# All sixteen shift and scale sums of the first modulation on VectorE, low-part products one group later, and the third chunk's low weights on VectorE

## The chip, the cores and the metric

The kernel runs on one core of one Trainium2 chip. The metric is the device time of one execution in microseconds (us); lower is better. TensorE is PE in the profile, VectorE DVE, ScalarE ACT, GpSimd POOL, and SyncE (SP) issues the loads.

## The reference

One layer of a streaming encoder over 1024 tokens of width 1024, all in f32. What matters here is its beginning:

```
mod = silu(c) @ w_ada + b_ada            # six vectors of 1024: sh1, sc1, gt1, sh2, sc2, gt2
h   = rms_norm(x, g_pre_mix) * (1 + sc1) + sh1
zin = h @ w_in                           # 1024 x 3072, the combined input projection
```

After it come a gated depthwise convolution over 31 taps, a chunkwise gated recurrence of four heads, the output projection, and a SwiGLU feed-forward part with its own modulation. The change touches only what is quoted.

## The kernel before

**The start stage.** `x` lies as eight tiles of 128 tokens. For each block `kt` of 128 channels (eight of them) the kernel needs one column of scale and one of shift: the dot product of `silu(c)` with a tile of `w_ada` of 128 channels by 1024. A tile of scale is multiplied and summed by VectorE (`scale(kt)`, one instruction that also accumulates). A tile of shift is treated likewise by `shift(kt)` for kt 0, 4, 5, 6 and 7. For kt 1, 2 and 3 (`TURNED_SHIFTS`) the tile is stored the other way round in HBM, and TensorE makes the column with eight matmuls of one column each (`shift_by_columns`), into a PSUM bank. `scale_shift(kt)` then makes the gain `gs` and the bias `mod` of the block (both of one column).

**Groups.** The normalised x is turned by TensorE in sixteen groups (`turn_x(g)`, four transposes of 128x128 each), a group being one block of channels by half of the tokens. `GROUPS` orders them: g 0 to 2 are kt 0 to 2 for the first half of the tokens, g 3 to 5 the same for the second half, and from g 6 on both halves of kt 3, of kt 4, and so on. For each group ScalarE applies gain and bias from PSUM and then rounds to the high part (`full_and_high(g)`, which signals `hi_ready`), VectorE subtracts to get the low part (`low_half(g)`, which signals `h_ready`), and TensorE adds the group's products for the first two chunks of `w_in` into `pair[0]` and `pair[1]` (`project_group(g)`). A product of two f32 numbers is made of three matmuls of 512 columns: high by high, high weight by low x, low weight by high x; with two chunks that is six matmuls a group, all after `h_ready`.

**Order on each engine** is the order of the program. ScalarE makes the squares and root mean squares of the x tiles (`squares`), tiles 0 to 3 ahead of group 0, tile 4 behind group 1, tiles 5 to 7 behind group 2. VectorE scales each x tile by them (`normalise_x`). `other_vectors()` on VectorE copies the turned small vectors out of `bank(3)`, which is the half of `pair[1]` that the second half of the tokens uses; it brings `vec_ready` to 2. TensorE waits for `vec_ready` 2 ahead of group 3. GpSimd splits the first two chunks' weights and, behind them, the third's (`split_first`).

**After the start stage** TensorE goes straight on: `project_first()` is the third chunk of `w_in` (48 matmuls, into `pair[3]`), and then chunk by chunk the rest of the kernel.

Of the kernel before, what the change touches and what calls it, by code (L numbers as in the profile page):

```python
# [26 lines left out]
P = 128  # L27
# [54 lines left out]
TURNED_SHIFTS = (1, 2, 3)  # L82
# [111 lines left out]
def build(nc, t_in, out):  # L194
# [11 lines left out]
    with ctx:  # L206
# [26 lines left out]
        cond_col = keep("cond_col", [P, KT])  # L233
# [68 lines left out]
        shift_column = sem("shift_column")  # L302
# [100 lines left out]

        def column_bank(kt):

            return bank(1 if kt == TURNED_SHIFTS[0] else 7)

# [356 lines left out]
        def _(pool):  # L764
# [91 lines left out]
            for q in range(2):  # L856
                split_first(2, q)
# [169 lines left out]
        def _(act):  # L1027
# [20 lines left out]
            act.wait_ge(vec_ready, 1)  # L1048
            act.activation(cond_col[:, :], vec[:, ROW_C:ROW_C + KT], ACT.Silu).then_inc(cond_ready, 1)
# [35 lines left out]
            squares(range(4, 5))  # L1085
            full_and_high(2)
            squares(range(5, TT))
            for g in range(EARLY, 16):
                full_and_high(g)
# [353 lines left out]
        def _(dve):  # L1443
# [16 lines left out]
            def lower_bounds():  # L1460

                dve.wait_ge(cond_ready, 3)
# [28 lines left out]
            def scale_shift(kt):  # L1491
# [5 lines left out]
                turned_here = sum(n <= kt for n in TURNED_SHIFTS)  # L1497
                if kt in TURNED_SHIFTS:
                    dve.wait_ge(shift_column, turned_here)
                    src = column_bank(kt)[:, kt:kt + 1]  # L1500
                else:
                    dve.wait_ge(shift_summed, kt + 1 - turned_here)
                    src = sums0[:, 1, kt:kt + 1]
                dve.tensor_tensor(mod[:, kt:kt + 1], src, vec[:, ROW_BADA + kt:ROW_BADA + kt + 1], ALU.add
# [17 lines left out]

            def normalise_x(i):

                dve.wait_ge(ss_ready, i + 1)
                normalise(x0[:, i, :], x0[:, i, :], i, 0).then_inc(xs_ready, 1)
# [9 lines left out]
            low_half(0)  # L1536
            scale_shift(1)
            scale(2)
            low_half(1)
            scale_shift(2)  # L1540
            other_vectors()
            low_half(2)
            for i in range(4, TT):
                normalise_x(i)
            scale(3)
            low_half(3)
            scale_shift(3)
# [4 lines left out]
            scale_shift(4)  # L1552
            for kt in range(3, KT):
# [4 lines left out]
                if kt + 2 < KT:  # L1558
                    shift(kt + 2)
                    scale_shift(kt + 2)  # L1560
            dve.memset(u[:, 0:TAPS - 1], 0.0)
# [484 lines left out]
        def _(pe):  # L2046
# [29 lines left out]
            def project_group(g):  # L2076
# [4 lines left out]
                hi, lo = (ha_hi, ha_lo) if kt < 4 else (hb_hi, hb_lo)  # L2081
                pe.wait_ge(h_ready, g + 1)
# [366 lines left out]
```

## Time and profile before

| | |
|---|---|
| median of 3 runs | 1116.43 us (1115.89 to 1846.04) |
| the profiled execution, its time | 1116.59 us |
| its span | 1114.8 us |
| TensorE busy | 1086.9 us, 97% of the span |
| VectorE, ScalarE, GpSimd busy | 828.2, 491.6, 746.2 us |
| chain of waits, share of TensorE | 94% |
| data moved | 108.02 MB, mean 97 GB/s |

The span is the part of the time between the first and the last instruction of the trace. The busy times of the engines overlap.

### The profile page before, as it was taken

The page shows a single profiled execution, that of the slowest core. Times are in us where ns is not written, and L with a number is a line of the kernel's source. Part 1 is how long each engine was busy: PE and PEld are TensorE (multiplying, and loading weights), DVE is VectorE, ACT ScalarE, POOL GpSimd, SP SyncE. Part 2 cuts the span into 40 slices and gives each one's busy share as a digit, 9 for nine tenths or more (in the row PEclk, how much of TensorE's full clock was granted, in tenths as well). Part 3 has the DMA queues.
Part 4 walks back from the last instruction along what each step waited for, and adds up shares of the span by engine and source line. Part 5 has one row for each costly group of instructions (what it writes and reads, how often), then busy time and mean ns, then how long its engine had stood idle before and what let it go on. Part 6 is the DMA issues. An engine that isn't in the chain of part 4 may idle for free.

```text
span 1114.8 us, 14441 instructions
## 1 busy us (share of the span) xinstructions
PE 1086.9 (97%) x5091; PEld 903.9 (81%) x5091; DVE 828.2 (74%) x1173; ACT 491.6 (44%) x833; POOL 746.2 (67%) x643
## 2 busy tenths in 40 slices
PE   4999999999999999999999999999999999999996
PEld 4788888888878888888888888888888888888885
DVE  4977997979997885689675757575766666666658
ACT  4765474564743734345333333332333333332324
POOL 5559648566572820438977777777786868696966
PEclk9999999999999999999999999999999999999999
DMA  9633313331211481303222222222221212222227
GB/s 350 221 103 124 96 57 95 95 96 56 61 55 39 170 320 57 114 25 98 66 76 67 76 66 72 61 69 65 76 67 61 73 60 74 65 66 69 65 53 297
DMA packets 98794, 108.02 MB, mean 97 GB/s; under 512 B 6590, under 2 KB 76451, under 8 KB 98723
## 3 DMA queue, kind: packets, MB, share of 16 engines
q1 hardware_dynamic: 97264, 102.79, 28.6%
q10 hardware_dynamic: 1458, 4.31, 1.0%
q8 instruction: 41, 0.67, 0.3%
q14 instruction: 31, 0.25, 0.1%
HBM read 98.68 MB, written 8.40 MB: 96 GB/s over the span
## 4 chain that ended last, share of the span: by engine, by line
PE 94%; DVE 3%; DMA 1%; issue 1%; ACT 1%; SPq 0%; DVEq 0%; ACTq 0%
PE pair L2335 34%; PE pair L2132 23%; PE pair L2355 17%; PE pair L2244 8%; PE pair L2174 2%; PE pair L2298 2%; PE pair L2378 2%; PE pair L2089 1%; DMA x<-in_x 1%; PE pair L2169 1%; PE pair L2188 1%; PE pair L2061 1%; PE pair L2100 1%; PE pair L2190 1%; PE pair L2183 1%
## 5 line engine op out<-in xcount | busy, mean ns | idle before, releaser
L1931 DVE TENSOR_TENSOR yt<-yt,pair 128x512 f32<-128x512 f32 x264 | 176.0, 683 | 34.7 <-PE pair L2355 34.7
L1607 DVE SCALAR_TENSOR_TENSOR pair<-u,conv_w_col,pair 128x512 f32<-128x512 f32 x208 | 139.5, 746 | 2.1 <-ACT pair L1203 1.6
L922 POOL TENSOR_TENSOR raw_r<-raw,w_hi 128x512 fp32r<-128x512 f32 x68 | 96.2, 1415 | 65.2 <-ACT w_hi L1341 65.2
L822 POOL TENSOR_TENSOR ada<-ada,cond 128x256 f32<-128x256 f32 x96 | 78.5, 852 | 70.4 <-DMA ada<-in_w_ada 70.3
L2355 PE MATMUL pair<-w_hi,op_hi 128*128 128x512 f32 x280 | 109.0, 389 | 0.0
L2355 PE MATMUL pair<-w_lo,op_hi 128*128 128x512 f32 x280 | 109.0, 389 | 0.0
L2355 PE MATMUL pair<-w_hi,op_lo 128*128 128x512 f32 x280 | 108.9, 389 | 0.0
L931 POOL TENSOR_TENSOR w_lo<-w_lo_f,w_hi 128x512 fp32r<-128x512 f32 x70 | 95.1, 1359 | 0.0
L2335 PE MATMUL pair<-t_lo,w_hi 128*128 128x512 f32 x240 | 93.7, 390 | 0.0
L2335 PE MATMUL pair<-t_hi,w_hi 128*128 128x512 f32 x240 | 93.4, 389 | 0.0
L812 POOL TENSOR_TENSOR w_lo<-raw,w_hi 128x256 fp32r<-128x256 f32 x84 | 66.8, 826 | 27.6 <-ACT w_hi L1098 27.5
L1341 ACT ACTIVATE w_hi<-raw 128x512 fp32r<-128x512 f32 x68 | 42.5, 626 | 73.0 <-PE pair L2335 71.7
L2335 PE MATMUL pair<-hb_lo,w_hi 128*128 128x512 f32 x160 | 63.1, 394 | 0.0
L2335 PE MATMUL pair<-hb_hi,w_hi 128*128 128x512 f32 x160 | 62.6, 391 | 0.0
L2132 PE MATMUL pair<-ha_hi,w_hi 128*128 128x512 f32 x192 | 62.4, 406 | 0.0
L2335 PE MATMUL pair<-ha_lo,w_hi 128*128 128x512 f32 x160 | 62.3, 390 | 0.0
L2335 PE MATMUL pair<-ha_hi,w_hi 128*128 128x512 f32 x160 | 62.3, 389 | 0.0
L2132 PE MATMUL pair<-hb_hi,w_hi 128*128 128x512 f32 x192 | 62.0, 404 | 0.0
L2355 PEld LDWEIGHTS pair<-w_hi,op_hi 128*128 128x128 f32 x280 | 52.6, 188 | 11.4
L2355 PEld LDWEIGHTS pair<-w_lo,op_hi 128*128 128x128 f32 x280 | 52.6, 188 | 11.0
L2355 PEld LDWEIGHTS pair<-w_hi,op_lo 128*128 128x128 f32 x280 | 52.6, 188 | 11.0
L2132 PE MATMUL pair<-ha_lo,w_hi 128*128 128x512 f32 x192 | 59.5, 391 | 0.0
(338 smaller groups left out, 2955.2 us busy)
## 6 DMA issues: line engine op xcount, KB each, us to landing
ada<-in_w_ada SPq DMA_DIRECT2D x40, 512.0 KB, 4.8
raw<-in_w_ffn_in SPq DMA_DIRECT2D x56, 256.0 KB, 2.9
raw<-in_w_in SPq DMA_DIRECT2D x21, 512.0 KB, 4.8
w_lo_f<-in_w_ffn_out SPq DMA_DIRECT2D x40, 256.0 KB, 3.1
w_hi_f<-in_w_ffn_out SPq DMA_DIRECT2D x30, 256.0 KB, 3.1
x<-in_x SPq DMA_DIRECT2D x8, 512.0 KB, 10.2
raw<-in_w_out SPq DMA_DIRECT2D x8, 512.0 KB, 3.4
ada_late<-in_w_ada SPq DMA_DIRECT2D x8, 512.0 KB, 6.9
```

The lines of the kernel that those rows point to most:

```text
L812: i_ = pool.tensor_tensor(w_lo[:, g % WS, cols], raw[:, g % RAW, cols], w_hi[:, g % WS, cols], ALU.subtract)
L822: i_ = pool.tensor_tensor(ada[:, n % ADA_RING, cols], ada[:, n % ADA_RING, cols], cond[:, cols], ALU.mult)
L922: pool.tensor_tensor(place_part(at), place_full(at), place_part(GU_HIGH[m % 3]), ALU.subtract).then_inc(gu_low, 1)
L931: pool.tensor_tensor(place_part(at), place_full(at), place_part(DOWN_HIGH[d % 2]), ALU.subtract).then_inc(down_low, 1)
L1341: act.activation(place_part(GU_HIGH[m % 3]), place_full(WEIGHT_PLACES[e][k]), ACT.Copy).then_inc(gu_high, 1)
L1607: i_ = dve.scalar_tensor_tensor(out=dst, in0=tap_of(j + 1, h), scalar=tap_weight(j + 1, t), in1=dst, op0=ALU.mult, op1=ALU.add)
L1931: i_ = dve.tensor_tensor(dst, dst, bank(4 + t), ALU.add)
L2132: i_ = pe.matmul(dst[:, cols], w, x[:, cols], start=first and s_ == 0, stop=last and s_ == 2)
L2174: i_ = pe.matmul(dst[:, cols(i)], keys[:, half % 2, cols(i)], right_queries(i, 1 << half), start=True, stop=True)
L2244: i_ = pe.matmul(dst[:, cols], x, w[:, cols], start=first and s_ == 0, stop=last and s_ == 2)
L2335: i_ = pe.matmul(dst, a[:, w], x[:, n, :], start=s in (0, 1, 3, 4) and n == 0 and s_ == 0, stop=n == 3 and s_ == 2, skip_group_check=True)
L2355: i_ = pe.matmul(bank(4 + t), x, w, start=q % 2 == 0 and s_ == 0, stop=s_ == 2, skip_group_check=True)
```

## The change

It does four things.

1. `TURNED_SHIFTS`, `shift_by_columns`, `cond_col` and `shift_column` go. VectorE runs `shift(1)`, `shift(2)` and `shift(3)` like the others; the tiles are stored like the others.
2. `project_group(g)` becomes `group_high(g)` (four matmuls, the two weights' high and low parts by the high part of x, after `hi_ready`) and `group_low(g)` (two matmuls by the low part of x, after `h_ready`). For groups 0 and 1 they follow one another. Group 2's low products come behind the turns of groups 3 to 5, and from group 4 on the low products of the group before come behind a group's high ones.
3. On ScalarE the squares of x tiles 4 to 7 all stand ahead of group 2. On VectorE `normalise_x(4)` stands ahead of `shift(2)`, tiles 5 to 7 ahead of `low_half(2)`, and `other_vectors()` moves from behind `scale_shift(2)` to behind `scale_shift(4)`.
4. GpSimd makes only the third chunk's high weights (two instructions); VectorE makes its low ones (`third_low_part`, two instructions behind `low_half(15)`). `project_first` runs its 32 products with the high weights first and its 16 with the low ones behind them.

```diff
@@ -79,7 +79,6 @@
 EARLY = 3
 GROUPS = ([(kt, half) for half in range(2) for kt in range(EARLY)]
           + [(kt, half) for kt in range(EARLY, KT) for half in range(2)])
-TURNED_SHIFTS = (1, 2, 3)
 LATE_TAPS = range(27, 31)
 LATE_SUMS = 2 * (len(LATE_TAPS) - 1)
 TAP_STEPS = 2 * (TAPS - len(LATE_TAPS))
...
@@ -854,7 +848,9 @@
                 split_first(g, 1)
             pool.wait_ge(ss_ready, TT)
             for q in range(2):
-                split_first(2, q)
+                pool.wait_ge(first_raw_loaded[2 * 2 + q], 16)
+                pool.tensor_copy(w_hi[:, 2, HALF_COLUMNS[q]], first_raw[:, 2, HALF_COLUMNS[q]]).then_inc(third_high, 1)
+            pool.wait_ge(w_split, WS)
             low(WS)
             pool.wait_ge(h_ready, 16)
             me.wait()
...
@@ -1045,8 +1041,6 @@
             act.dma_start(rows_b[:, :], t_in["conv_w"].rearrange("l j (t c) -> (l j t) c", c=P)).then_inc(vec_loaded, 16)
             act.wait_ge(c_loaded, 16)
             act.activation(cond[:, :], cond[:, :], ACT.Silu).then_inc(cond_ready, 1)
-            act.wait_ge(vec_ready, 1)
-            act.activation(cond_col[:, :], vec[:, ROW_C:ROW_C + KT], ACT.Silu).then_inc(cond_ready, 1)
             act.preload_act_table_set("sqrt_and_others")
             def hi_parts(call, full, groups):
                 for g in groups:
...
@@ -1082,10 +1076,8 @@
             act.activation(w_hi[:, 1, HALF_COLUMNS[0]], first_raw[:, 1, HALF_COLUMNS[0]], ACT.Copy).then_inc(first_high, 1)
             full_and_high(0)
             full_and_high(1)
-            squares(range(4, 5))
-            full_and_high(2)
-            squares(range(5, TT))
-            for g in range(EARLY, 16):
+            squares(range(4, TT))
+            for g in range(2, 16):
                 full_and_high(g)
             act.wait_ge(vec_ready, 2)
             act.activation(lb_tmp[:, 1, :], lb_tmp[:, 0, :], ACT.Exp).then_inc(cond_ready, 1)
...
@@ -1494,14 +1486,8 @@
                 dve.scalar_tensor_tensor(out=gs[:, 0, kt:kt + 1], in0=sums0[:, 0, kt:kt + 1],
                                          scalar=scale_bias[:, kt:kt + 1], in1=vec[:, ROW_GPRE1 + kt:ROW_GPRE1 + kt + 1],
                                          op0=ALU.add, op1=ALU.mult)
-                turned_here = sum(n <= kt for n in TURNED_SHIFTS)
-                if kt in TURNED_SHIFTS:
-                    dve.wait_ge(shift_column, turned_here)
-                    src = column_bank(kt)[:, kt:kt + 1]
-                else:
-                    dve.wait_ge(shift_summed, kt + 1 - turned_here)
-                    src = sums0[:, 1, kt:kt + 1]
-                dve.tensor_tensor(mod[:, kt:kt + 1], src, vec[:, ROW_BADA + kt:ROW_BADA + kt + 1], ALU.add
+                dve.wait_ge(shift_summed, kt + 1)
+                dve.tensor_tensor(mod[:, kt:kt + 1], sums0[:, 1, kt:kt + 1], vec[:, ROW_BADA + kt:ROW_BADA + kt + 1], ALU.add
                                   ).then_inc(mod0_ready, 1)
 
             def low_half(g):
...
@@ -1519,6 +1505,14 @@
                 cols = HALF_COLUMNS[0]
                 dve.tensor_tensor(w_lo[:, 1, cols], first_raw[:, 1, cols], w_hi[:, 1, cols], ALU.subtract
                                   ).then_inc(first_low, 1)
+
+            def third_low_part(q):
+
+                dve.wait_ge(third_high, q + 1)
+                cols = HALF_COLUMNS[q]
+                i_ = dve.tensor_tensor(w_lo[:, 2, cols], first_raw[:, 2, cols], w_hi[:, 2, cols], ALU.subtract)
+                if q:
+                    i_.then_inc(w_split, 1)
 
             def normalise_x(i):
 
...
@@ -1534,22 +1528,26 @@
             first_low_part()
             scale(1)
             low_half(0)
+            shift(1)
             scale_shift(1)
             scale(2)
             low_half(1)
+            normalise_x(4)
+            shift(2)
             scale_shift(2)
-            other_vectors()
+            for i in range(5, TT):
+                normalise_x(i)
             low_half(2)
-            for i in range(4, TT):
-                normalise_x(i)
             scale(3)
             low_half(3)
+            shift(3)
             scale_shift(3)
             low_half(4)
             scale(4)
             low_half(5)
             shift(4)
             scale_shift(4)
+            other_vectors()
             for kt in range(3, KT):
                 low_half(2 * kt)
                 if kt + 2 < KT:
...
@@ -1558,6 +1556,8 @@
                 if kt + 2 < KT:
                     shift(kt + 2)
                     scale_shift(kt + 2)
+            for q in range(2):
+                third_low_part(q)
             dve.memset(u[:, 0:TAPS - 1], 0.0)
             lower_bounds()
 
...
@@ -2073,33 +2073,32 @@
                                       ident[:, :])
                 i_.then_inc(turned, 1)
 
-            def project_group(g):
+            def group_high(g):
 
                 kt, half = GROUPS[g]
                 cols = slice(half * HALF, (half + 1) * HALF)
                 w = slice(kt * P, (kt + 1) * P)
-                hi, lo = (ha_hi, ha_lo) if kt < 4 else (hb_hi, hb_lo)
-                pe.wait_ge(h_ready, g + 1)
+                hi = ha_hi if kt < 4 else hb_hi
+                pe.wait_ge(hi_ready, g + 1)
                 for n in range(2):
                     if kt == 0:
                         pe.wait_ge(first_low if n else first_split, 1)
                     if kt == 4:
                         pe.wait_ge(w_split, n + 1)
-                    for s_, (a, b) in enumerate([(w_hi, hi), (w_hi, lo), (w_lo, hi)]):
-                        i_ = pe.matmul(pair[n][:, cols], a[:, n, w], b[:, kt % 4, cols], start=kt == 0 and s_ == 0,
-                                       stop=kt == KT - 1 and s_ == 2)
+                    for s_, a in enumerate([w_hi, w_lo]):
+                        pe.matmul(pair[n][:, cols], a[:, n, w], hi[:, kt % 4, cols], start=kt == 0 and s_ == 0, stop=False)
+
+            def group_low(g):
+
+                kt, half = GROUPS[g]
+                cols = slice(half * HALF, (half + 1) * HALF)
+                w = slice(kt * P, (kt + 1) * P)
+                lo = ha_lo if kt < 4 else hb_lo
+                pe.wait_ge(h_ready, g + 1)
+                for n in range(2):
+                    i_ = pe.matmul(pair[n][:, cols], w_hi[:, n, w], lo[:, kt % 4, cols], start=False, stop=kt == KT - 1)
                     if g == 2 * KT - 1:
                         i_.then_inc(w_used, 1)
-            def shift_by_columns(kt):
-
-                pe.wait_ge(cond_ready, 2)
-                pe.wait_ge(shift_loaded[kt], 16)
-                if kt == TURNED_SHIFTS[2]:
-                    pe.wait_ge(mod0_ready, TURNED_SHIFTS[1] + 1)
-                for k in range(KT):
-                    i_ = pe.matmul(column_bank(kt)[:, kt:kt + 1], shift_tile(kt)[:, k * P:(k + 1) * P], cond_col[:, k:k + 1],
-                                   start=k == 0, stop=k == KT - 1)
-                i_.then_inc(shift_column, 1)
 
             for g in range(3):
                 turn_x(g)
...
@@ -2107,20 +2106,21 @@
             pe.wait_ge(vec_ready, 1)
             pe.transpose(bank(3)[:, 0:ROWS], rows_a[:, :], ident[0:ROWS, 0:ROWS])
             pe.transpose(bank(3)[:, P:P + TAPS * CT], rows_b[:, :], ident[0:TAPS * CT, 0:TAPS * CT]).then_inc(vec_turned, 1)
-            shift_by_columns(1)
-            project_group(0)
-            shift_by_columns(2)
-            project_group(1)
-            project_group(2)
+            for g in range(2):
+                group_high(g)
+                group_low(g)
+            group_high(2)
             for g in range(3, 6):
                 turn_x(g)
-            shift_by_columns(3)
+            group_low(2)
+            pe.wait_ge(vec_ready, 2)
             for g in range(3, 16):
-                if g == 3:
-                    pe.wait_ge(vec_ready, 2)
-                project_group(g)
+                group_high(g)
+                if g > 3:
+                    group_low(g - 1)
                 if g + 3 < 16:
                     turn_x(g + 3)
+            group_low(15)
 
             def split_product(dst, slot, w_cols, x_hi, x_lo, first, last):
 
...
@@ -2142,11 +2142,19 @@
 
             def project_first():
 
+                pe.wait_ge(third_high, 2)
+                for kt in range(KT):
+                    hi, lo = (ha_hi, ha_lo) if kt < 4 else (hb_hi, hb_lo)
+                    for x in (hi, lo):
+                        for cols in HALF_COLUMNS:
+                            pe.matmul(pair[3][:, cols], w_hi[:, 2, kt * P:(kt + 1) * P], x[:, kt % 4, cols],
+                                      start=kt == 0 and x is hi, stop=False)
                 pe.wait_ge(w_split, WS)
                 for kt in range(KT):
-                    hi, lo = (ha_hi, ha_lo) if kt < 4 else (hb_hi, hb_lo)
-                    i_ = split_product(pair[3], 2, slice(kt * P, (kt + 1) * P), hi[:, kt % 4, :], lo[:, kt % 4, :],
-                                       kt == 0, kt == KT - 1)
+                    hi = ha_hi if kt < 4 else hb_hi
+                    for cols in HALF_COLUMNS:
+                        i_ = pe.matmul(pair[3][:, cols], w_lo[:, 2, kt * P:(kt + 1) * P], hi[:, kt % 4, cols], start=False,
+                                       stop=kt == KT - 1)
                 i_.then_inc(w_used, 1)
 
             def pe_slot(t, n):
```

Left out of the diff: the declarations of the tiles and semaphores that go or come, the count in the wait of `lower_bounds` (2 for 3), and the host's storing of the three shift tiles.

## Rows read from the trace of the kernel before

**Rows 1.** the page's part 1: busy us (share of the span), instructions

```profile
PE 1086.9 (97%) x5091; PEld 903.9 (81%) x5091; DVE 828.2 (74%) x1173; ACT 491.6 (44%) x833; POOL 746.2 (67%) x643
```

**Rows 2.** stretches: us, busy us of PE, PEld, DVE, ACT, POOL, granted clock

```profile
62.60:140.00 77.40, 77.40 (x382) 65.42 (x381) 67.02 (x103) 42.59 (x55) 59.74 (x74) 1.00 0.36 114
140.00:1114.80 974.80, 964.48 (x4500) 801.62 (x4498) 719.24 (x986) 409.52 (x716) 654.47 (x513) 1.00 0.27 85
```

**Rows 3.** waits of PE after 140 us: total us, times, longest

```profile
PE pair L2174 <- issue: 1.0, 3, 0.4
```

**Rows 4.** timeline of PE: start us, us, engine, line, operation, count

```profile
18.94 3.42 PE L2100 MATMUL pair<-cond_col,ada 128*128 128x1 f32 x16
...
35.98 1.84 PE L2100 MATMUL pair<-cond_col,ada 128*128 128x1 f32 x16
```

**Rows 5.** timeline of DVE, 22 to 29 us

```profile
22.39 0.16 DVE L1504 TENSOR_TENSOR mod<-pair,vec 128x1 f32<-128x1 f32 x1 [2.32 <-PE pair L2100]
...
28.37 0.16 DVE L1504 TENSOR_TENSOR mod<-pair,vec 128x1 f32<-128x1 f32 x1 [3.43 <-PE pair L2100]
28.44 0.19 DVE L1454 COPY vec<-pair 128x41 f32<-128x41 f32 x1
...
28.86 0.16 DVE L1458 TENSOR_TENSOR lb_tmp<-vec 128x4 f32<-128x4 f32 x1
```

**Rows 6.** timeline of DVE, sums and differences

```profile
19.26 0.68 DVE L1513 TENSOR_TENSOR ha_lo<-x,ha_hi 128x512 fp32r<-128x512 f32 x1
...
34.80 1.75 DVE L1481 SCALAR_TENSOR_TENSOR ada<-ada,cond 128x1024 f32<-128x1024 f32 x1
...
40.47 1.22 DVE L1488 SCALAR_TENSOR_TENSOR ada<-ada,cond 128x1024 f32<-128x1024 f32 x1
...
41.74 0.38 DVE L1504 TENSOR_TENSOR mod<-sums,vec 128x1 f32<-128x1 f32 x1
```

**Rows 7.** timeline of POOL

```profile
34.36 2.78 POOL L848 TENSOR_TENSOR w_lo<-first_raw,w_hi 128x256 fp32r<-128x256 f32 x2
```

**Rows 8.** timeline of ACT: modulation of a group, squares

```profile
22.65 0.78 ACT L1074 ACTIVATE x<-pair,mod,gs 128x512 f32<-128x512 f32 x1 [4.11 <-DVE mod L1504]
...
23.99 1.04 ACT L1031 ACTIVATE w_hi<-x 128x1024 fp32r<-128x1024 f32 x1
...
29.97 1.04 ACT L1031 ACTIVATE w_hi<-x 128x1024 fp32r<-128x1024 f32 x1
...
31.24 1.04 ACT L1031 ACTIVATE w_hi<-x 128x1024 fp32r<-128x1024 f32 x1
```

**Rows 9.** timeline of PE: turns, and groups 1 and 2

```profile
16.59 2.18 PE L2072 MATMUL pair<-ident,x 128*128 128x128 f32 x9 [1.35 <-DVE x L1474]
...
28.19 0.77 PE L2089 MATMUL pair<-ha_hi,w_hi 128*128 128x512 f32 x1
...
30.93 0.79 PE L2089 MATMUL pair<-ha_hi,w_hi 128*128 128x512 f32 x1
```

**Rows 10.** timeline of PE: groups 3, 4 and 15, then the next stage

```profile
37.79 0.47 PE L2089 MATMUL pair<-ha_hi,w_hi 128*128 128x512 f32 x1
...
39.61 0.48 PE L2089 MATMUL pair<-ha_hi,w_hi 128*128 128x512 f32 x1
...
61.22 0.39 PE L2089 MATMUL pair<-hb_hi,w_hi 128*128 128x512 f32 x1
...
62.58 0.62 PE L2132 MATMUL pair<-ha_hi,w_hi 128*128 128x512 f32 x2
```

**Rows 11.** line L614, the last x tile: issue, and us to landing

```profile
L614 SPq DMA_DIRECT2D x<-in_x x1: 432/432/432, 13.2 to 13.2; - x1
...
DMA to landing us min/median/max: 12.8/12.8/12.8
```

**Rows 12.** line L604, the shift tile of kt 3: issue, and us to landing

```profile
L604 SPq DMA_DIRECT2D ada<-in_w_ada x1: 432/432/432, 14.2 to 14.2; - x1
...
DMA to landing us min/median/max: 14.4/14.4/14.4
```

More of the change, by code:

```diff
@@ L232, in build @@
         sums0 = keep("sums0", [P, 2, KT])
-        cond_col = keep("cond_col", [P, KT])
         gs = keep("gs", [P, 2, KT])
@@ L301, in build @@
         shift_summed = sem("shift_summed")
-        shift_column = sem("shift_column")
+        third_high = sem("third_high")
         first_raw_loaded = [sem(f"first_raw_loaded{i}") for i in range(2 * WS)]
@@ L402, in first_tile @@
             return x0[:, 4 * half:4 * half + 4, kt * P:(kt + 1) * P]
-        def column_bank(kt):
-            return bank(1 if kt == TURNED_SHIFTS[0] else 7)
         def turns_of(src):
@@ L1460, in lower_bounds @@
             def lower_bounds():
-                dve.wait_ge(cond_ready, 3)
+                dve.wait_ge(cond_ready, 2)
                 me.done(dve.reciprocal(lb_tmp[:, 2, :], lb_tmp[:, 1, :]))
@@ L2437 @@
         if name == "w_ada":
-            rows = a[0]
-            a = np.array(a.transpose(0, 2, 1))
-            for n in TURNED_SHIFTS:
-                block = rows[:, n * P:(n + 1) * P].reshape(KT, P, P)
-                a[0, n * P:(n + 1) * P, :] = block.transpose(1, 0, 2).reshape(P, D)
+            a = np.ascontiguousarray(a.transpose(0, 2, 1))
         arrays[f"in_{name}"] = a
```

## The prediction

> **What bounds the kernel now.** I read the page first. TensorE is busy for 97% of the span [rows 1]. The reader should then ask where TensorE is *not* busy, and whether later stages could swallow a shift of the first one. The stretches answer this: from 62.60 to 140 us TensorE is busy in all of the 77.40 us, and from 140 to the end it lacks about 10 us of 974.80 [rows 2], of which the waits name little; the largest group is 1.0 us [rows 3]. So whatever moves the end of the start stage moves the end of the kernel by as much. That stage ends where the third chunk's first product starts, at 62.58 us [rows 10]. All that the change touches lies ahead of that point, except the order of the third chunk's products. I therefore walk the engines' timelines from 19 us on, in the new program order.
>
> **What is removed.** On TensorE three series of column products: 3.42 us for kt 1, the same for kt 2, and 1.84 us for kt 3 [rows 4], 8.7 us in all. VectorE waited for the first two, 2.32 and 3.43 us [rows 5]. If nothing took their place the kernel would win most of 8 us.
>
> **What is added on VectorE.** Three sums of 1024 columns. One takes 1.22 us when GpSimd is idle and 1.75 when GpSimd works beside it [rows 6, 7]: the 1.75 us one at 34.80 overlaps GpSimd's subtraction from 34.36 on. The next instruction starts some 0.08 us before an end, so I take 1.14 or 1.68 a sum. From a sum's start to a finished `mod` is 40.47 to about 41.9, 1.45 us [rows 6] (the 0.38 us that the last small operation shows overlaps; the next one starts at once). A difference of 512 columns costs 0.61 of its 0.68 us [rows 6], up to 0.8 beside GpSimd.
>
> **Groups 0 to 2.** VectorE ends `low_half(0)` at 19.87 (19.26 + 0.61) and runs `shift(1)` at once: `mod` 1 stands at 21.3 instead of 22.55 [rows 5, 6]. ScalarE then needs 1.44 us for gain and high part of group 1, as from 22.65, and goes on with squares 1.34 us after its start (22.65 to 23.99) [rows 8]. So high part 1 is ready at 22.85 and the squares start at 22.75. They are four now, 1.27 us each (29.97 to 31.24) [rows 8]; the last x tile lands at 13.2 + 12.8 = 26.0 [rows 11], in time for the fourth. ScalarE is free for group 2 at 22.75 + 5.1 = 27.85, so high part 2 is ready at 29.3. `mod` 2 is earlier than that: x tile 4 is scaled by about 25.05 and `shift(2)` adds 1.45, 26.5. Here the squares are late next, and of 28.37 + 0.16 for `mod` 2 in the kernel before [rows 5] little is won. TensorE has groups 0 and 1 done at about 21.7 and 25.6 (six products take 2.74 us there, 28.19 to 30.93 [rows 9]) and waits for group 2 until 29.3. The squares moved forward cost nothing by themselves: in the kernel before, three of them stood behind group 2.
>
> **Turns of groups 3 to 5.** High products of group 2: 4 x 0.457 = 1.8 us at that pace, or 0.9 at the pace of 61.22 to 62.58 (six in 1.36 us) [rows 9, 10]. I take the slow one, since TensorE waits 3.7 us ahead of it: 31.1. A turn is 0.243 us (nine in 2.18, [rows 9]), four 0.97: group 3 is turned at 32.1, group 5 at 34.0. Low products of group 2: until 34.9.
>
> **The added wait.** `other_vectors()` sets `vec_ready` to 2 and TensorE waits for it ahead of group 3. It stood behind `scale_shift(2)`, done at 29.02 [rows 5], and hid there; now it is behind `scale_shift(4)`. Queued behind TensorE's wait are all products from group 3 on and turn 6, on which high part 6 and `low_half(6)` hang. VectorE has ahead of it, from `low_half(2)` at 29.9: `scale(3)` beside GpSimd, 31.6; `low_half(3)`, which needs turn 3 (32.1) and 1.44 us of ScalarE, 33.55 to 34.2; `shift(3)`, whose tile landed by 14.2 + 14.4 = 28.6 [rows 12], and `mod` 3, 2.0 us beside GpSimd, 36.2; `low_half(4)` 0.8, 37.0; `scale(4)` 1.14, `low_half(5)` 0.61, `shift(4)` and `mod` 4 1.45, 40.2; `other_vectors()` 0.58 (28.44 to 29.02, [rows 5]), 40.8. TensorE has nothing to do from 34.9 to 40.8 and starts group 3 at 40.8, where the kernel before starts it at 37.79 [rows 10]. That is the step on which the sign rests: three freed stretches of TensorE, and a start of group 3 that is 3.0 us later.
>
> **From group 3 to 15.** A group with its turn is 1.83 us (37.79 to 39.61), one without 1.36 [rows 10]: 10 x 1.83 + 3 x 1.36 = 22.4. The kernel before took 24.8 us, 37.79 to 62.58 [rows 10], so it lost 2.4 to waits for `low_half`. These go: the high products wait for the high part only, the low ones come a group later, and `mod` 3 and 4 are ready when group 3 starts. For each further block VectorE needs 2 x 1.14 + 2 x 0.61 + 0.3 = 3.8 us without GpSimd, TensorE 2 x 1.83 = 3.7. GpSimd ends its high weights a few us after 41 and has nothing else, since the third chunk's low parts (2.78 us a half [rows 7]) are gone. VectorE keeps up: by this pace the last `mod` is ready about 57.6, high part 15 by 60.5, both before TensorE asks. So 40.8 + 22.4 = 63.2.
>
> **The pace after the wait.** The price nobody sees in the program is TensorE's clock. Six products took 2.74 us at 28.19 and 1.36 us at 61.22, and column products 3.42 and then 1.84 [rows 4, 9, 10]: in the kernel before, the lower level (1.2 GHz) held from 16.59 to about 31 and the upper one (2.4 GHz) from there, while the granted clock is 1.00 in the stretches after it [rows 2]. After 5.9 us of nothing TensorE may start group 3 at the lower level. Bounds: nothing, if the level stays up; at the other end the 14.4 us that the start took, half of which is lost, 7.2. The dense stretch ahead of the rise began at 28.19 and lasted about 3 us. That is the nearest row, but the column products before it may have helped, so I take somewhat more, 4.4 us at the lower level, half of which is lost: 2.2. The end of the stage is 65.4, +2.8.
> The Trainium skill, "TensorE: Matmul & The Clock Gate", Part 1, says that the throttled clock is the default and that idleness brings it back. No row here shows a fall. By that rule the sum is the one above with its 2.2 us, without it 63.2.
>
> **The third chunk.** The same 48 products in another order; VectorE's two differences (2 x 0.61) end near 62.5, the first product that reads them is 32 products later, 7 us of cover. If that cover went it would be 1.2 us. Nothing, then; nor do the removed 5.5 us on GpSimd count, which had nothing waiting. ScalarE loses one small operation ahead of a wait for x.
>
> **Sum.** Profiled execution 1116.59 + 2.8 = 1119.4; the median of the runs is 0.16 lower, so 1119.2.
>
> **The rivals.** *The level holds, or VectorE's sums fall cheap.* TensorE resumes at the upper level, or reaches it in groups 0 to 1, which brings turn 3 and with it the wait 1.4 us forward: 61.8 to 63.2, -0.8 to +0.6, 1116.2 mid. For it: nothing in the trace shows a fall. Against it: the products at 28.19, with no gap before them, are still slow. Chance 0.26.
> *The gain arrives.* If the wait for `vec_ready` were met early, group 3 would start at 34.9, and VectorE's chain would set the end: `mod` 4 at 40.2, three blocks more at 3.8, 51.6, then 3.5 us for ScalarE and `low_half` 14 and 15 and 1.4 of products, and some 2 us of lower clock, about 59: -3.6, 1112.8. Against it stands the order in VectorE's program, which is plain. Chance 0.05.
> *Slower by the clock alone.* The short stretches with waits between them could keep TensorE at 1.2 GHz as long as at the start, 14.4 us from 40.8, and it decides as soon as the level is still low at about 47: 65.4 + 5 = 70.4, +7.8, 1124.2. Against it: groups 3 to 15 hold no column products, which filled much of the slow time. Chance 0.08.
> *The chain of differences takes over.* If VectorE's sums cost 1.68 throughout, a block is 5.1 us, `mod` 7 comes 3.9 us later, at 61.5, and group 15 ends about 67: +4.4, 1120.8. Against it: the 1.22 us sums fall where GpSimd is idle [rows 6, 7]. It lies inside the forecast's spread. Chance 0.06.
>
> **How the numbers follow.** Forecast 0.55, centre 1119.2, own spread 1117.5 to 1121.5 (lower level for 3.5 to 7 us, VectorE's sums with or without GpSimd). The rivals as given, 0.45 together. The range takes in the first rival and the last, and stops short of the gain and of the long lower clock, 0.13. Their ends are 1115.6 and 1122.3; I set them 1.2 us further out, for the spread of the runs (0.7 us between the two lower times and the profiled one) and for VectorE's chain ahead of group 3, which holds three sums at either price (0.54 us each): 1114.4 to 1123.5. A measurement of this kernel can tell about 2% from no change, 22 us; no case above reaches a third of that. What is left for either side is mostly what the one time of 1846.04 hints at, and a misreading. Faster 0.01, same 0.97, slower 0.02.
>
> **What would show it.** In the timeline of TensorE: no column products; a gap of some 6 us ahead of group 3's first product, released by VectorE's `lb_tmp` subtraction of `other_vectors()`; that product at 40 to 41 us; about 0.43 us from product to product behind it and 0.23 some us later; no waits between groups 3 and 15; the first product of chunk 3 at 65.4. On VectorE `mod` 1 at 21.3 and `mod` 2 at 26.5; on ScalarE four squares in a row from 22.8. It is wrong if group 3 starts before 39 us, if the pace there is 0.23 from the first product, or if a later stage has lost what the start lost.

## The result, and the profile after

Over eleven executions the changed kernel takes 1119.69 us (1118.51 to 1120.5), the kernel before 1116.53 us in as many: a ratio of 1.0026, 95% interval [1.0016, 1.0036]. The profiled execution took 1118.81 us, 0.9 us under the median; its span is 1117.1 us, 2.3 us more than before. (Ratios here leave out single disturbed executions; of before, 1846.04 and 6273.03 us.)

The page of the changed kernel, its row of TensorE's busy time and the granted clock over the 40 slices of the span:

```profile
PE 1078.8 (97%) x5043; PEld 896.9 (80%) x5043; DVE 831.3 (74%) x1181; ACT 491.1 (44%) x832; POOL 738.8 (66%) x637
...
PEclk9799999999999999999999999999999999999999
```

TensorE is busy for 8.1 us *less* than before [rows 1], much as the removed column products of 8.7 us say, and the kernel is longer. So TensorE must stand idle for some 10 us more. The stretches show where (columns: length, busy time of PE, PEld, DVE, ACT, POOL, granted clock, share of DMA, GB/s):

```profile
16.00:31.00 15.00, 8.04 (x27) 6.32 (x28) 13.58 (x26) 9.51 (x19) 3.54 (x4) 0.88 1.04 394
31.00:41.00 10.00, 3.56 (x15) 2.89 (x13) 7.49 (x18) 4.00 (x6) 5.51 (x7) 0.67 1.05 392
41.00:48.00 7.00, 6.99 (x30) 5.81 (x31) 2.28 (x4) 2.93 (x5) 1.23 (x2) 0.76 0.62 156
48.00:58.00 10.00, 10.00 (x55) 8.29 (x54) 9.59 (x22) 7.89 (x12) 0.00 (x0) 1.00 0.01 2
58.00:140.00 82.00, 82.00 (x402) 69.08 (x401) 68.80 (x109) 45.87 (x60) 58.23 (x71) 1.00 0.34 105
140.00:1100.00 960.00, 958.20 (x4480) 797.35 (x4479) 708.59 (x973) 405.58 (x704) 646.03 (x511) 1.00 0.27 83
```

Two stretches hold the idle time, 16 to 31 us (7 us idle) and 31 to 41 us (6.4 us). From 48 to 140 us there is none, and from 140 to 1100 us it is 1.8 us, where the kernel before has 1.6. Note the granted clock: 0.67 and 0.76 of full speed from 31 to 48 us.

The timeline of TensorE, which answers to [rows 4, 9, 10]:

```profile
18.79 0.78 PE L2089 MATMUL pair<-ha_hi,w_hi 128*128 128x512 f32 x1
...
22.86 0.50 PE L2089 MATMUL pair<-ha_hi,w_hi 128*128 128x512 f32 x1 [1.62 <-ACT ha_hi L1072]
23.20 0.40 PE L2089 MATMUL pair<-ha_hi,w_lo 128*128 128x512 f32 x1
...
29.29 0.80 PE L2089 MATMUL pair<-ha_hi,w_hi 128*128 128x512 f32 x1 [4.77 <-ACT ha_hi L1072]
...
31.16 2.76 PE L2072 MATMUL pair<-ident,x 128*128 128x128 f32 x12
33.57 0.99 PE L2099 MATMUL pair<-ha_lo,w_hi 128*128 128x512 f32 x2
41.01 0.80 PE L2089 MATMUL pair<-ha_hi,w_hi 128*128 128x512 f32 x1 [6.44 <-DVE lb_tmp L1450]
41.60 0.63 PE L2089 MATMUL pair<-ha_hi,w_lo 128*128 128x512 f32 x1
...
42.88 1.05 PE L2072 MATMUL pair<-ident,x 128*128 128x128 f32 x4
...
44.52 0.40 PE L2089 MATMUL pair<-ha_hi,w_hi 128*128 128x512 f32 x1
...
65.07 0.62 PE L2150 MATMUL pair<-ha_hi,w_hi 128*128 128x512 f32 x2
```

No row of column products is left. The reader is to see three things. First, the two idle times in brackets: 4.77 us ahead of group 2's high part, released by ScalarE, and 6.44 us ahead of group 3's first product, released by VectorE's `lb_tmp`, the last instruction of `other_vectors()`. Group 3 starts at 41.01 us, in the kernel before at 37.79 [rows 10]. Secondly, the distance of starts: 0.43 us from 41.60 on (the lower level; the granted clock reads 0.50 from 41 to 44 us), 0.23 us at 44.52. Thirdly, between 41.01 and 65.07 us the timeline has no bracket: the waits of groups 8 and 9 for low parts are gone. In the kernel before they were these:

```profile
48.08 0.50 PE L2089 MATMUL pair<-hb_hi,w_hi 128*128 128x512 f32 x1 [0.73 <-DVE hb_lo L1513]
...
50.89 0.50 PE L2089 MATMUL pair<-hb_hi,w_hi 128*128 128x512 f32 x1 [0.71 <-DVE hb_lo L1513]
```

The stage ends at 65.07 us, before it ended at 62.58 [rows 10]: +2.5 us, of which the span shows 2.3.

The list of TensorE's waits up to 66 us names the same two, the second together with one of 1.62 us ahead of group 1 (total us, times, longest):

```profile
PE pair L2089 <- DVE lb_tmp L1450: 6.4, 1, 6.4
PE pair L2089 <- ACT ha_hi L1072: 6.4, 2, 4.8
```

VectorE's timeline shows its side [rows 5, 6]:

```profile
21.13 0.14 DVE L1490 TENSOR_TENSOR mod<-sums,vec 128x1 f32<-128x1 f32 x1
...
26.26 0.15 DVE L1490 TENSOR_TENSOR mod<-sums,vec 128x1 f32<-128x1 f32 x1
...
34.33 1.75 DVE L1480 SCALAR_TENSOR_TENSOR ada<-ada,cond 128x1024 f32<-128x1024 f32 x1
...
36.02 0.67 DVE L1486 SCALAR_TENSOR_TENSOR gs<-sums,scale_bias,vec 128x1 f32<-128x1 f32 x1
...
40.31 0.14 DVE L1490 TENSOR_TENSOR mod<-sums,vec 128x1 f32<-128x1 f32 x1
...
40.79 0.16 DVE L1450 TENSOR_TENSOR lb_tmp<-vec 128x4 f32<-128x4 f32 x1
45.45 0.69 DVE L1499 TENSOR_TENSOR ha_lo<-x,ha_hi 128x512 fp32r<-128x512 f32 x1 [4.50 <-ACT ha_hi L1072]
```

`mod` 1 stands at 21.3 us (22.55 before) and `mod` 2 at 26.4 (28.5 before): the sums are faster than the column products were. But `other_vectors()` comes only at 40.4 to 40.95 us, and then VectorE itself has nothing to do for 4.50 us, because turn 6 was queued behind TensorE's wait. ScalarE's timeline has the four squares in a row from 22.71 us, and high part 2 ready behind them [rows 8]:

```profile
22.71 1.04 ACT L1027 ACTIVATE w_hi<-x 128x1024 fp32r<-128x1024 f32 x1
...
28.60 0.63 ACT L1072 ACTIVATE ha_hi<-x 128x512 fp32r<-128x512 f32 x1
```

### The profile page after: what moved, and what is told of

The parts are those of the page before. It is cut to its first block, busy times and chain, and to the rows that moved or that the text cites. A ratio compares the mean times of both kernels' runs of the same rounds, so it can differ in the third digit from the quotient of the medians.

```text
span 1117.1 us, 14344 instructions
## 1 busy us (share of the span) xinstructions
PE 1078.8 (97%) x5043; PEld 896.9 (80%) x5043; DVE 831.3 (74%) x1181; ACT 491.1 (44%) x832; POOL 738.8 (66%) x637
## 4 chain that ended last, share of the span: by engine, by line
PE 92%; DVE 3%; issue 2%; ACT 1%; DMA 1%; SPq 0%; DVEq 0%; ACTq 0%
PE pair L2343 34%; PE pair L2132 22%; PE pair L2363 17%; PE pair L2252 8%; PE pair L2182 2%; PE pair L2306 2%; PE pair L2089 1%; DMA x<-in_x 1%; PE pair L2150 1%; PE pair L2177 1%; PE pair L2196 1%; PE pair L2061 1%; PE pair L2198 1%; PE pair L2191 1%; PE pair L2099 1%
## 5 line engine op out<-in xcount | busy, mean ns | idle before, releaser
L927 POOL TENSOR_TENSOR w_lo<-w_lo_f,w_hi 128x512 fp32r<-128x512 f32 x70 | 95.4, 1363 | 0.0
L2343 PE MATMUL pair<-ha_lo,w_hi 128*128 128x512 f32 x160 | 62.3, 390 | 0.0
L2343 PE MATMUL pair<-ha_hi,w_hi 128*128 128x512 f32 x160 | 62.3, 389 | 0.0
L2343 PE MATMUL pair<-hb_hi,w_hi 128*128 128x512 f32 x160 | 62.2, 389 | 0.0
L2132 PE MATMUL pair<-ha_hi,w_hi 128*128 128x512 f32 x184 | 60.0, 407 | 0.0
L2132 PE MATMUL pair<-hb_hi,w_hi 128*128 128x512 f32 x184 | 59.5, 405 | 0.0
L918 POOL TENSOR_TENSOR w_lo<-w_lo_f,w_hi 128x512 fp32r<-128x512 f32 x36 | 48.0, 1337 | 15.9 <-ACT w_hi L1333 15.9
```

Of the source, the lines that this page charges most:

```text
L918: pool.tensor_tensor(place_part(at), place_full(at), place_part(GU_HIGH[m % 3]), ALU.subtract).then_inc(gu_low, 1)
L927: pool.tensor_tensor(place_part(at), place_full(at), place_part(DOWN_HIGH[d % 2]), ALU.subtract).then_inc(down_low, 1)
L2132: i_ = pe.matmul(dst[:, cols], w, x[:, cols], start=first and s_ == 0, stop=last and s_ == 2)
L2343: i_ = pe.matmul(dst, a[:, w], x[:, n, :], start=s in (0, 1, 3, 4) and n == 0 and s_ == 0, stop=n == 3 and s_ == 2, skip_group_check=True)
```

## The experiments

The end of the start stage below is the first product of the third chunk in each profile. The span minus this end is 1050.9 to 1052.3 us in all twelve kernels, so the end of the stage tells the time to within some 1.4 us, and a smaller difference of two stage ends need not show in the time. Each profile is of one execution. The ratios are to executions of the kernel before that were taken beside each kernel; their medians lie between 1116.47 and 1116.81 us, so medians of different rows compare to about 0.3 us.

| kernel | first product of group 3 | stage ends | span | median of runs | ratio to before, 95% |
|---|---|---|---|---|---|
| before | 37.79 | 62.58 | 1114.8 | 1116.53 | 1 |
| changed | 41.01 | 65.07 | 1117.1 | 1119.69 | 1.0026 [1.0016, 1.0036] |
| before_vectors_late | 42.02 | 66.13 | 1117.9 | 1120.2 | 1.0036 [1.0024, 1.0049] |
| filled_wait | 41.19 | 63.72 | 1115.5 | 1117.28 | 1.0005 [0.9996, 1.0014] |
| vectors_early | 34.12 | 57.67 | 1109.5 | 1110.61 | 0.9946 [0.9932, 0.996] |
| early_filled | 32.59 | 57.00 | 1109.0 | 1110.56 | 0.9948 [0.9935, 0.996] |
| sums_only | 34.15 | 61.36 | 1113.2 | 1114.82 | 0.9986 [0.9977, 0.9995] |
| split_only | 38.09 | 60.96 | 1112.8 | 1115.65 | 0.9998 [0.9988, 1.0007] |
| early_third_pool | 33.83 | 59.38 | 1111.7 | 1113.1 | 0.9966 [0.9955, 0.9978] |
| early_last_square | 33.32 | 56.78 | 1107.9 | 1110.32 | 0.9944 [0.9932, 0.9955] |
| early_columns | 35.21 | 57.67 | 1109.8 | 1111.74 | 0.9954 [0.994, 0.9968] |
| last_square_filled | 33.03 | 57.06 | 1108.0 | 1110.15 | 0.9938 [0.9925, 0.9951] |

The theory is the prediction's: the wait for `vec_ready`, moved behind `scale_shift(4)`, costs what the rest of the change wins, and TensorE's clock takes some more.

**The moved wait alone, taken back: vectors_early.**

```diff
             scale_shift(2)
+            other_vectors()
...
             scale_shift(4)
-            other_vectors()
```

> The changed kernel with other_vectors() back behind scale_shift(2), nothing else. Theory (the moved wait costs the most): group 3 starts near 34.6 us instead of 41.01, released by ScalarE's high part 3 or by TensorE's own work, and the stage ends near 59 to 60 us instead of 65.07; time 1113.8 us, 0.995 of the changed kernel, 0.9975 of the kernel before. Rival (VectorE's chain of sums would hold TensorE anyway, the wait only shows it): waits of 4 us or more appear between groups 3 and 15 and the time stays at 1118.5 or above.

```profile
29.62 0.80 PE L2089 MATMUL pair<-ha_hi,w_hi 128*128 128x512 f32 x1 [3.50 <-ACT ha_hi L1072]
...
31.49 2.18 PE L2072 MATMUL pair<-ident,x 128*128 128x128 f32 x12
...
34.12 0.47 PE L2089 MATMUL pair<-ha_hi,w_hi 128*128 128x512 f32 x1
...
45.99 0.73 PE L2099 MATMUL pair<-hb_lo,w_hi 128*128 128x512 f32 x2 [0.19 <-DVE hb_lo L1499]
...
54.31 0.50 PE L2089 MATMUL pair<-hb_hi,w_hi 128*128 128x512 f32 x1 [0.20 <-ACT hb_hi L1072]
...
57.67 0.62 PE L2150 MATMUL pair<-ha_hi,w_hi 128*128 128x512 f32 x2
```

The wait is gone, group 3 follows group 2's low products at 34.12 us, and the stage ends 7.4 us earlier; the median is 9.1 us under that of the changed kernel and 6.2 us under that of the kernel before taken beside it. (The spans of the two profiled executions differ by 7.6 us: one lies 0.9 us under its median, the other 0.8 above.) The waits that the rival asked for are 0.19 and 0.20 us. The rival fell. The expectation missed the size: the stage ends 1.3 us ahead of the nearer end of its 59 to 60, and the time is 3.2 us under its 1113.8. The prediction's walk for this case had 2 us of a lower clock behind group 3; here TensorE works without a gap from 29.62 us on and is at the upper level at group 3 (0.23 us between starts).

**The moved wait alone, in the kernel before: before_vectors_late.**

```diff
             scale_shift(2)
-            other_vectors()
             low_half(2)
...
             scale_shift(4)
+            other_vectors()
```

> The kernel before with other_vectors() moved behind scale_shift(4), nothing else. Theory: scale_shift(4) ended at 42.1 us, 0.6 us of other_vectors() no longer lie ahead of it, so vec_ready is 2 at about 42.1 and group 3 starts there instead of at 37.79: +3.9 to +4.3 us and up to 2 more where TensorE starts at the lower level; its waits for low parts (2.4 us) go in return: 1118.5 to 1120.5. Rival (the place of other_vectors() costs nothing in itself): 1116.5, within 0.3.

```profile
42.02 0.80 PE L2089 MATMUL pair<-ha_hi,w_hi 128*128 128x512 f32 x1 [4.54 <-DVE lb_tmp L1458]
42.61 0.63 PE L2089 MATMUL pair<-ha_lo,w_hi 128*128 128x512 f32 x1
...
45.82 0.40 PE L2089 MATMUL pair<-ha_lo,w_hi 128*128 128x512 f32 x1
```

Group 3 starts at 42.02 us after 4.54 us of waiting for `lb_tmp`, at the lower level (0.43 us between starts, 0.23 from 45.8 us), and the stage ends 3.55 us later. The median is 3.4 us over that of the kernel before taken beside it (1120.2 and 1116.81). The place of `other_vectors()` costs this in itself, without anything else of the change. The rival fell here too.

**The clock: filled_wait and early_filled.** Both put unused products into an idle bank where TensorE waits, 22 of them ahead of group 3 in the changed kernel, 18 ahead of group 2 in vectors_early.

```diff
+            for _ in range(22):
+                pe.matmul(bank(7), w_hi[:, 0, 0:P], ha_hi[:, 0, 0:HALF], start=True, stop=True)
             pe.wait_ge(vec_ready, 2)
```

> The changed kernel with 22 unused products of 512 columns into an idle PSUM bank ahead of TensorE's wait for vec_ready, so that TensorE is not idle there. Theory (the idle 6.4 us put the clock down): products of group 3 follow each other in 0.23 us instead of 0.43 from the first on; the lower level lasted from 41.01 to about 44.5 us, so 1.7 us are won: 1118.0. Rival (the level would be low anyway or costs nothing): the time of the changed kernel, 1119.7.

```profile
34.73 5.17 PE L2117 MATMUL pair<-ha_hi,w_hi 128*128 128x512 f32 x22
41.19 0.50 PE L2089 MATMUL pair<-ha_hi,w_hi 128*128 128x512 f32 x1 [1.29 <-DVE lb_tmp L1450]
41.53 0.40 PE L2089 MATMUL pair<-ha_hi,w_lo 128*128 128x512 f32 x1
```

The 22 products take 5.17 us, and group 3 starts 0.18 us later than in the changed kernel, yet its products follow one another in 0.23 us. (Of the 0.18 us, 0.16 are there at group 2 already, 29.45 and 29.29 us, ahead of the filling.) The stage ends 1.35 us earlier, and the time is 2.4 us less by the medians. So 1.35 us of the stage (1.5 us from group 3's start) is what the idle TensorE's clock costs, by the one profile of each; the other 1 us of the medians no profile shows.

> The kernel vectors_early with 18 unused products ahead of the high products of group 2, where TensorE waits from 24.5 to 29.3 us. Theory: groups 2 and 3 and the turns between them run at the upper level (0.12 us a turn, not 0.23; 0.23 a product, not 0.43), turn 3 ends 1.4 us earlier and the start of group 3 comes forward by as much: 1111.5 to 1112.5, 1.5 to 2 us under vectors_early. Rival (ScalarE's and VectorE's chains set the end of the stage once the wait is gone): within 0.5 us of vectors_early.

```profile
45.35 0.74 PE L2099 MATMUL pair<-hb_lo,w_hi 128*128 128x512 f32 x2 [0.48 <-DVE hb_lo L1499]
...
53.68 0.50 PE L2089 MATMUL pair<-hb_hi,w_hi 128*128 128x512 f32 x1 [0.20 <-ACT hb_hi L1072]
```

Group 3 starts 1.5 us earlier than in vectors_early, at 32.59 us, as expected. Only 0.7 us of it is left at the end of the stage and nothing in the medians (1110.56 against 1110.61 us). The rival holds: TensorE now waits for VectorE (0.16 us at 38.94 and 0.48 us at 45.35) and for ScalarE (0.20 us). So without the moved wait VectorE's chain is next, and ScalarE's close behind.

**The parts alone, on the kernel before: sums_only and split_only.** In sums_only the column products of TensorE go and `shift(1)`, `shift(2)`, `shift(3)` come, behind `low_half` 0, 1 and 3. In split_only `project_group` becomes `group_high` and `group_low`, with the column products left in. Their core:

```diff
-TURNED_SHIFTS = (1, 2, 3)
+TURNED_SHIFTS = ()
...
-            shift_by_columns(1)
             project_group(0)
-            shift_by_columns(2)
```

```diff
             for g in range(3, 16):
-                project_group(g)
+                group_high(g)
+                if g > 3:
+                    group_low(g - 1)
```

> The kernel before with the three shift columns summed by VectorE and TensorE's column products gone; nothing else is changed (other_vectors() stays behind scale_shift(2), a group's six products stay together, the squares stay where they were). Theory: group 3 starts when the turns of x tiles 4 to 7 are done, near 34.5 us instead of 37.79, but from group 8 on TensorE still waits for VectorE's differences, whose chain comes only 1.7 us earlier (mod 4 at 40.4 instead of 42.1): 1.5 to 3.5 us won, 1114 us. Rival (VectorE becomes the bound with 3.7 us more work): no gain, 1116.5.

> The kernel before with group_high and group_low in place of project_group (low products one group later from group 3 on), column products of TensorE kept. Theory: it takes only the waits for low parts between groups 3 and 15, 2.4 us at most, and some of them become waits for the high part: 1 to 2.4 us won, 1114.8 us. Rival (the waits only move on to ScalarE's high parts): 1116.5.

TensorE's timeline of sums_only:

```profile
34.15 0.77 PE L2088 MATMUL pair<-ha_hi,w_hi 128*128 128x512 f32 x1 [1.64 <-issue]
34.71 0.63 PE L2088 MATMUL pair<-ha_lo,w_hi 128*128 128x512 f32 x1
35.14 0.63 PE L2088 MATMUL pair<-ha_hi,w_lo 128*128 128x512 f32 x1
...
40.97 0.39 PE L2088 MATMUL pair<-ha_lo,w_hi 128*128 128x512 f32 x1
41.20 0.40 PE L2088 MATMUL pair<-ha_hi,w_lo 128*128 128x512 f32 x1
```

With the sums alone group 3 starts at 34.15 us, 3.6 us earlier, and at the end of the stage 1.2 us of it is left. Most of the rest went to the clock: the level had fallen, behind idle times of 0.76 and 0.94 us among the turns and 1.64 us ahead of group 3 (where VectorE's `low_half(3)` ends at 34.04 us), and groups 3 and 4 ran at 0.43 us between starts (0.23 from 40.97 on). With their turns they took 6.51 us, where two groups at the upper level take 3.66: 2.85 us. And TensorE waits 0.18 and 0.72 us for low parts again. The ratio is 0.9986, [0.9977, 0.9995]: a gain of 0.6 to 2.6 us, not the whole of what group 3 gained. What the sums would give at the upper level no run shows. With the split alone the profile has no wait of TensorE between groups 3 and 15, and the stage ends 1.6 us earlier; the medians are unclear, 0.9998 [0.9988, 1.0007]. Its twelve executions explain part of that: eight lie at 1114.6 to 1116.2 us with a mean granted clock of 0.996 to 0.998, three at 1117.27 to 1119.14 with 0.991 to 0.993, and one of 1118.43 with 0.998 does not fit. So the split's gain is shown in the profile and not in the median.

**The third chunk's low weights: early_third_pool.** vectors_early with GpSimd making them again, and the third chunk's products waiting for all of its weights.

```diff
             for q in range(2):
-                pool.wait_ge(first_raw_loaded[2 * 2 + q], 16)
-                pool.tensor_copy(w_hi[:, 2, HALF_COLUMNS[q]], first_raw[:, 2, HALF_COLUMNS[q]]).then_inc(third_high, 1)
+                split_first(2, q)
...
-            for q in range(2):
-                third_low_part(q)
```

> The kernel vectors_early with the third chunk's low weights back on GpSimd and the third chunk's products waiting for all of its weights. Theory: nothing waits for them in either form, but GpSimd then works beside VectorE's sums from 41.7 to 50 us (1.75 us a sum instead of 1.22), some 2 us of a chain that has little room left, since TensorE waits for VectorE and ScalarE by 0.2 us in vectors_early: 0.5 to 2 us slower than vectors_early. Rival (only VectorE's two more differences count): within 0.5 us of vectors_early.

GpSimd's, VectorE's and TensorE's timelines of this kernel, in that order:

```profile
44.58 2.89 POOL L842 TENSOR_TENSOR w_lo<-first_raw,w_hi 128x256 fp32r<-128x256 f32 x2
...
49.70 2.87 POOL L842 TENSOR_TENSOR w_lo<-first_raw,w_hi 128x256 fp32r<-128x256 f32 x2
```

```profile
45.11 1.76 DVE L1471 SCALAR_TENSOR_TENSOR ada<-ada,cond 128x1024 f32<-128x1024 f32 x1
...
50.22 1.75 DVE L1471 SCALAR_TENSOR_TENSOR ada<-ada,cond 128x1024 f32<-128x1024 f32 x1
```

```profile
48.08 0.73 PE L2095 MATMUL pair<-hb_lo,w_hi 128*128 128x512 f32 x2 [0.70 <-DVE hb_lo L1497]
...
53.17 0.73 PE L2095 MATMUL pair<-hb_lo,w_hi 128*128 128x512 f32 x2 [0.69 <-DVE hb_lo L1497]
```

VectorE's sums that start beside GpSimd's subtractions take 1.75 us instead of 1.22, and TensorE now waits 0.70 and 0.69 us for VectorE. The stage ends 1.7 us later and the median is 2.5 us up, a little beyond the 0.5 to 2 of the theory; the two intervals overlap by 0.0005, and all five executions lie above all five of vectors_early. The theory holds: this part of the change, for which the prediction's sum has no term, is worth some 2 us once VectorE's chain is next.

**What is next late: early_last_square and last_square_filled.**

```diff
-            squares(range(4, TT))
-            for g in range(2, 16):
+            squares(range(4, TT - 1))
+            full_and_high(2)
+            squares(range(TT - 1, TT))
+            for g in range(EARLY, 16):
```

On VectorE `normalise_x(7)` goes behind `low_half(2)`. The second kernel adds 6 unused products ahead of group 2.

> The kernel vectors_early with ScalarE's square of the last x tile moved behind group 2's high part, and VectorE's scaling of that tile behind low_half(2). Theory (the four squares in a row are what group 2 waits for): high part 2 is ready 1.3 us earlier, at 28.0 us, the turns of group 3 follow at once, and the stage ends 0.7 to 1.3 us earlier: 1109.6 us. Rival (VectorE's chain of sums sets the end now, as early_filled suggests, where a faster TensorE gained 0.05 us): within 0.4 us of vectors_early.

> The kernel early_last_square with 6 unused products between groups 1 and 2. Theory (from group 3 on TensorE now sits at VectorE's and ScalarE's heels, so a higher level early on is not passed on): within 0.4 us of early_last_square, 1110.0 to 1110.6, with less spread between runs. Rival (the lower level of groups 2 and 3 is still on the path): 1 us or more under early_last_square.

Group 2 starts 1.6 us earlier than in vectors_early (28.03 against 29.62 us) and the stage ends 0.9 us earlier, but the medians differ by 0.3 us, within the interval. The two theories can't be told apart at this size. With the filling nothing more is won, as expected. With vectors_early and early_filled these are the lowest kernels of the study, 0.9938 to 0.9948 of the kernel before, and not to be told from one another; the plain vectors_early is the simplest of them.

**The sums, on top of the rest: early_columns.** vectors_early with `TURNED_SHIFTS`, `shift_by_columns` and the two series ahead of groups 0 and 1 and the third ahead of group 3.

> The kernel vectors_early with the three shift columns back on TensorE (eight matmuls of one column each), everything else as there. Theory (VectorE's sums are worth the time that group 2 and group 3 come earlier): mod 2 comes back to about 28.4 us, group 2 waits until 29.9, and the columns of kt 3 cost 1.8 us ahead of group 3, which starts near 36.5 instead of 34.1: the stage ends 1.5 to 2.5 us later, time 1112.5 us. Rival (with the squares in a row the sums win nothing, since group 2 waits for ScalarE in both): within 0.5 us of vectors_early, 1110.8.

```profile
24.72 3.41 PE L2123 MATMUL pair<-cond_col,ada 128*128 128x1 f32 x16
...
33.51 1.84 PE L2123 MATMUL pair<-cond_col,ada 128*128 128x1 f32 x16
35.21 0.48 PE L2102 MATMUL pair<-ha_hi,w_hi 128*128 128x512 f32 x1
```

Neither theory nor rival was right. Group 3 starts 1.1 us later than in vectors_early, the stage ends at the same 57.67 us in this profile, and the median is 1.1 us higher with intervals that overlap ([0.994, 0.9968] and [0.9932, 0.996]). The column products keep TensorE busy where it otherwise waits, and it reaches the upper level at about 31 us, so that between group 3 and the end of the stage it takes 22.5 us, against 23.6 in vectors_early. So about 1 us of the gain of vectors_early comes from moving the sums to VectorE by the medians and nothing by the ends of the stage; whether it is above nothing stays open.

## Why the prediction was right

**What bounds the kernel.** Confirmed: the end of the stage moved by 2.5 us and the span by 2.3, with TensorE fully busy from 48 to 140 us. Over all twelve kernels the later part of the span varies by 1.4 us.

**Groups 0 to 2.** `mod` 1 at 21.3, squares from 22.7, high part 2 at 29.2, group 2 at 29.29 us: within 0.1 us of the walk. `mod` 2 was 0.1 us earlier than said.

**The added wait.** Group 3 was put at 40.8 us and started at 41.01; TensorE's idle time at 5.9 us and was 6.44. The step on which the sign rested is right, and the two experiments that move `other_vectors()` alone, one in each direction, show it as the cause: +3.5 us of stage in the kernel before, -7.4 in the changed one. The walk charged `low_half(4)` 0.2 us too much and the small operations behind `shift(3)`, of which one took 0.67 us beside GpSimd, 0.3 too little. Its 0.8 us for a difference beside GpSimd is no upper price: the kernel before has one of 1.21 us at 43.99 us.

**From group 3 to 15.** 22.4 us at the upper level was the term; with filled_wait, which has it, 41.19 to 63.72 is 22.5 us. No waits, as said. The 2.4 us that the kernel before was said to lose to waits are 1.4 us in the two that its trace names; split_only, without them, takes 22.9 us from group 3 on.

**The pace after the wait.** 2.2 us were put in; the changed kernel took 24.06 us from group 3 on, so 1.5 to 1.6 us were lost, and filled_wait gave 1.35 us of stage back. The lower level lasted to about 44.5 us, 3.5 us, not 4.4. The mechanism is right, the term 0.6 to 0.7 us too large. Together with the 0.2 us of the start this makes 65.07 for the 65.4 that was forecast. By the rule of the Trainium skill ("TensorE: Matmul & The Clock Gate", Part 1), that idleness brings the lower clock back, the trace agrees: 0.23 us between starts at 23.20, 0.43 from 29.88 on, after 4.77 us of idle time.

One thing the walk had wrong: it held TensorE at the lower level through groups 0 and 1. The level rose within group 0 (0.43 us between starts at 19.79, 0.24 at 20.60), was still the upper one behind a wait of 1.62 us, and fell back ahead of group 2. Groups 0 and 1 were done at 21.2 and 24.5 us, not 21.7 and 25.6, which only made the wait for group 2 longer, and the turns ran at the low pace all the same (12 in 2.76 us). That this did no harm to the forecast is luck.

**The third chunk.** It was costed at nothing with 7 us of cover, and so far as its own products go that held. That GpSimd, freed, makes VectorE's sums faster was in the walk (3.8 us a block); the price without it stands only in the last rival (5.1 us a block, +4.4 us), and it is 1.7 us of stage in early_third_pool. In the changed kernel it was not put back alone.

**The time.** 1119.2 us forecast, 1119.69 measured; the profiled execution 1119.4 and 1118.81. The walk gave the stage 0.3 us too much, and the median was put 0.16 us under the profiled execution, where it came out 0.9 above: two errors of opposite sign, so the nearness of the median is in part luck. The sign and the 2.5 us of the stage are not. (The 1122.3 us that the upper end of the range starts from is worked out nowhere in the prediction.)

**The rivals.** *The gain arrives* (1112.8) is what vectors_early did, at 1110.61: the walk for it carried 2 us of a lower clock that did not come. *The level holds* is what filled_wait forces: 1117.28, 1.1 us over the 1116.2 given as its middle, with a stage end of 63.72 beyond the 63.2 of its upper bound. The long lower clock and the long chain did not come; the longest lower level behind group 3's start is that of sums_only, some 6 us.

## What to carry to other kernels

A wait that is met early in the old order is free and shows in no row of the profile; when the instructions that meet it are moved, walk both engines from the wait on, and list all that stands ahead of the signal. Here three instructions of 0.6 us in all were moved behind eighteen others, and a change that took 8.7 us of work from TensorE ended its first stage 2.5 us later. Look for the small side job that guards a buffer, not only for the large one that fills it.

## What the runs showed of the hardware

The granted clock of the profile reads 1.00 in the kernel before from 16 to 31 us, while six products took 2.74 us there [rows 9], the pace of 1.2 GHz; in the changed kernel it reads 0.67 from 31 to 41 us. It seems to tell the level only once it has risen for the first time; the distance of starts tells it from the beginning.

When it first rises does not follow from the program alone. The kernel before and before_vectors_late have the same instructions on TensorE, column products too. In the one the level was still the lower at 30.93 us; in the other the second series of column products took 2.10 us instead of 3.41, from 24.55 us on, and the products behind it were 0.23 us apart. So the rows don't show that column products keep the level low. In the changed kernel it rose near 20.5 us, in vectors_early the products were 0.43 us apart until 31.07.

And the level is not the same in each execution of one program: the twelve of split_only, 1114.6 to 1119.14 us, mostly go with their mean granted clock, 0.998 to 0.991.
